# A hybrid S5 and gated-linear-attention step in float32: the loads that bring the gates back move from ScalarE's queue to SyncE's, and two GLA branch tiles take turns with the low parts of S5's output

## What is computed

```python
h = rmsnorm(x, g_mix)
z = h @ w_in        # [u_s5 | q | k | v | r | a_lowrank | gate_s5 | gate_gla]
y5 = s5_mixer(u, ...)                       # diagonal complex state
z5 = gelu(y5);  o5 = z5 * sigmoid(z5 @ w_s5_glu)
og = rmsnorm_per_head(gla_mixer(q, k, v, ...)) * silu(r)
merged = sigmoid(gate_s5) * (o5 @ w_s5_br) + sigmoid(gate_gla) * (og @ w_gla_br)
x = x + merged @ w_out
x = x + square(relu(rmsnorm(x, g_ffn) @ w_ff1)) @ w_ff2
y = rmsnorm(x, g_final)                     # plus the new S5 and GLA states
```

## Time and profile before

| | us |
|---|---|
| median of 3 timed executions | 3113.45 |
| lowest, highest | 3100.98, 3114.78 |
| the profiled execution, its own time | 3107.87 |
| its span, first to last instruction | 3106.1 |
| PE busy (share) | 2974.8 (96%) |
| DVE busy | 1346.8 (43%) |
| POOL busy | 1166.3 (38%) |
| ACT busy | 508.3 (16%) |

### The profile page before, as it was taken

How to read it: one execution, slowest core, us unless ns; L and a number is a source line. 1 busy time by engine, 2 the same in 40 slices (tenths; PEclk the granted TensorE clock), 3 DMA queues, 4 the chain that set the end, 5 groups by cost and what they waited for, 6 DMA issues and landing times.

```text
span 3106.1 us, 47026 instructions
## 1 busy us (share of the span) xinstructions
PE 2974.8 (96%) x19152; PEld 2884.8 (93%) x19152; DVE 1346.8 (43%) x2545; ACT 508.3 (16%) x812; POOL 1166.3 (38%) x917
## 2 busy tenths in 40 slices
PE   5999999889999999999999999998899999999997
PEld 5999988789999999999999999888899999999997
DVE  6645546544353233333463254563534333323334
ACT  3222221231210000000232222213111000000001
POOL 3433322244454443444443332223444443444341
PEclk9999989899999999999999999999999999999998
DMA  3232324422111111111213232444211111111112
GB/s 127 93 113 76 67 86 131 161 99 88 41 51 45 48 45 48 45 48 45 100 52 118 56 78 47 130 131 169 89 52 45 48 46 47 45 48 45 48 45 74
DMA packets 116627, 230.87 MB, mean 74 GB/s; under 512 B 11953, under 2 KB 37329, under 8 KB 115281
## 3 DMA queue, kind: packets, MB, share of 16 engines
q1 hardware_dynamic: 65664, 119.57, 13.3%
q10 hardware_dynamic: 50768, 108.41, 11.0%
HBM read 183.84 MB, written 44.09 MB: 73 GB/s over the span
## 4 chain that ended last, share of the span: by engine, by line
PE 92%; DVE 3%; ACT 2%; ACTq 1%; issue 1%; DMA 0%; DVEq 0%
PE ps L448 28%; PE ps L449 27%; PE ps L450 27%; PE ps L590 2%; PE ps L646 1%; PE ps L667 1%; PE ps L668 1%; PE ps L645 1%; DVE f_h L1339 1%; PE ps L656 1%; PE ps L669 0%; DVE r_o L1339 0%; DVE f_o L1339 0%; PE ps L496 0%; ACTq L1179 0%
## 5 line engine op out<-in xcount | busy, mean ns | idle before, releaser
L430 POOL TENSOR_TENSOR w_hi<-w_raw,zero 128x512 fp32r<-128x512 f32 x456 | 529.3, 1161 | 1829.7 <-PE ps L450 1817.7
L448 PE MATMUL ps<-r_h,w_hi 128*128 128x344 f32 (+1 forms) x2736 | 893.0, 326 | 30.9 <-DVE f_o L1339 15.1
L450 PE MATMUL ps<-r_h,w_lo 128*128 128x344 f32 (+1 forms) x2736 | 882.1, 322 | 0.0
L449 PE MATMUL ps<-r_o,w_hi 128*128 128x352 f32 (+1 forms) x2280 | 735.8, 323 | 0.0
L432 POOL TENSOR_TENSOR w_lo<-w_raw,w_hi 128x512 fp32r<-128x512 f32 x456 | 639.6, 1403 | 64.8
L448 PE MATMUL ps<-r_z,w_hi 128*128 128x344 f32 (+1 forms) x1776 | 583.9, 329 | 25.2 <-DVE f_h L1339 18.5
L449 PE MATMUL ps<-r_h,w_hi 128*128 128x344 f32 (+1 forms) x1800 | 583.0, 324 | 0.0
L450 PE MATMUL ps<-r_z,w_lo 128*128 128x344 f32 (+1 forms) x1776 | 575.2, 324 | 0.0
L448 PEld LDWEIGHTS ps<-r_h,w_hi 128*128 128x128 f32 x2736 | 519.4, 190 | 41.2 <-issue 17.6
L450 PEld LDWEIGHTS ps<-r_h,w_lo 128*128 128x128 f32 x2736 | 519.1, 190 | 0.0
L449 PE MATMUL ps<-r_m,w_hi 128*128 128x344 f32 (+1 forms) x1392 | 449.1, 323 | 0.0
(11 more groups left out here) (337 smaller groups left out, 2727.6 us busy)
## 6 DMA issues: line engine op xcount, KB each, us to landing
w_raw<-wpack SPq DMA_DIRECT2D x456, 256.0 KB, 2.7
f_z<-s_constants ACTq DMA_DIRECT2D x16, 514.0 KB, 3.8
f_h<-s_constants ACTq DMA_DIRECT2D x16, 514.0 KB, 3.8
f_h<-xT ACTq DMA_DIRECT2D x4, 1040.0 KB, 9.0
gate_s_scratch<-f_o ACTq DMA_DIRECT2D x8, 520.0 KB, 3.3
gate_gla_scratch<-f_o ACTq DMA_DIRECT2D x8, 520.0 KB, 3.4
f_h<-gate_gla_scratch ACTq DMA_DIRECT2D x8, 520.0 KB, 8.0
f_h<-gate_s_scratch ACTq DMA_DIRECT2D x8, 520.0 KB, 15.0
```

Source lines behind the costliest of these rows:

```text
L430: pool.tensor_tensor(w_hi[:, s, :], raw, zero[:, :].to_broadcast([P, WB]), ALU.subtract)
L448: pe.matmul(out, wh, h, start=first, stop=False)
L449: pe.matmul(out, wh, l, start=False, stop=False)
L450: return pe.matmul(out, wl, h, start=False, stop=last)
```

## The change

SP takes over the 16 loads of the gates. It issues them once per half, in front of the weight block with the index `JOB_FIRST[JOB["bg", 0]] + RING`, that is the first block behind those of bg 0 to 3, the block of glu 0. Ahead of them it waits for gg 7's last matmul and for all gate stores. ACT no longer waits for these nor issues the loads; its `y_load(3)` and its wait for the y stores stay. On DVE, `gla_branch` is split into one function per block. Where o5_low(0), o5_low(1), gla_branch(4), o5_low(2), o5_low(3), gla_branch(5) stood, the order is now block 0 of bg 4, o5_low(0), block 1, o5_low(1), block 2, o5_low(2), block 0 of bg 5, o5_low(3), blocks 1 and 2; the waits for gg 4 and gg 5 come first.

```diff
--- before.py
+++ after.py
@@ -404,8 +404,21 @@
 
         @block.sync
         def _(sp):
+
+            def gates_back(half):
+                sp.wait_ge(*job_used(half, ("gg", KT_D - 1)))
+                for s in range(2):
+                    sp.wait_ge(gg_stored[s], (half + 1) * 4 * 16)
+                    sp.wait_ge(gs_stored[s], (half + 1) * 4 * 16)
+                for m in range(KT_D):
+                    sp.dma_start(ft(X_LO[half], m), gg_dram[m]).then_inc(gg_landed[m], 16)
+                for m in range(KT_D):
+                    sp.dma_start(ft(X_HI[half], m), gs_dram[m]).then_inc(gs_landed[m], 16)
+
             for half in range(HALVES):
                 for i in range(IT_FF * RING):
+                    if i == JOB_FIRST[JOB["bg", 0]] + RING:
+                        gates_back(half)
                     g = half * HALF_BLOCKS + i
                     if g >= RAW:
                         sp.wait_ge(w_split[(g - RAW) % RING], (g - RAW) // RING + 1)
@@ -1163,26 +1176,13 @@
                         if t == OG_HIGH[h]:
                             act.wait_ge(ocols_read, (half + 1) * PARTS)
                             act.activation(rt(QKV[half] + Q_V, h), r_tile(half, h), ACT.Copy).then_inc(hi_ready, 1)
-                act.wait_ge(*job_used(half, ("gg", KT_D - 1)))
-                gates_back(half, range(1))
                 act.wait_ge(s5dec_ready, half + 1)
                 act.dma_start(s5_dec_out[half], s5_new[:, :, :, :]).then_inc(s5dec_stored, 16)
-
-
-            def gates_back(half, gla, s5=()):
-                for s in range(2):
-                    act.wait_ge(gg_stored[s], (half + 1) * 4 * 16)
-                    act.wait_ge(gs_stored[s], (half + 1) * 4 * 16)
-                for m in gla:
-                    act.dma_start(ft(X_LO[half], m), gg_dram[m]).then_inc(gg_landed[m], 16)
-                for m in s5:
-                    act.dma_start(ft(X_HI[half], m), gs_dram[m]).then_inc(gs_landed[m], 16)
 
             def branches(half):
                 for m in range(KT_S):
                     if m == 1:
                         y_load(half, KT_S - 1)
-                        gates_back(half, range(1, KT_D), range(KT_D))
                     act.wait_ge(yperm_landed[m], (half + 1) * 16)
                     z = ft(WORK[half], m)
                     yp = fv(SIDE[half] + S_Y + m * J * YC, J * YC).rearrange("p (j c) -> p j c", j=J)
@@ -1784,14 +1784,16 @@
                 tt(nim, nim, t1, ALU.add).then_inc(s5dec_ready, 1)
 
             def branches(half):
+                def gla_block(m, b):
+                    (c0, cn), gate, job = BLK[b], ft(X_LO[half], m), ("bg", m)
+                    block_done(half, job, b)
+                    tt(gate[:, c0:c0 + cn], gate[:, c0:c0 + cn], ps[:, block_bank(job, b), 0:cn], ALU.mult
+                       ).then_inc(block_read(half, job, b)[0], 1)
+
                 def gla_branch(m):
                     dve.wait_ge(gg_landed[m], (half + 1) * 16)
-                    gate = ft(X_LO[half], m)
-                    for b, (c0, cn) in enumerate(BLK):
-                        job = ("bg", m)
-                        block_done(half, job, b)
-                        tt(gate[:, c0:c0 + cn], gate[:, c0:c0 + cn], ps[:, block_bank(job, b), 0:cn], ALU.mult
-                           ).then_inc(block_read(half, job, b)[0], 1)
+                    for b in range(len(BLK)):
+                        gla_block(m, b)
 
                 def s5_branch(m):
                     dve.wait_ge(gs_ready, half * KT_D + m + 1)
@@ -1825,12 +1827,12 @@
                     dve.wait_ge(*block_read(half, ("glu", m), 1))
                     dve.wait_ge(*block_read(half, ("glu", m), 2))
                     tt(ft(WORK[half], m), ft(WORK[half], m), ft(A_G, m % 2), ALU.mult).then_inc(full_ready, 1)
-                o5_low(0)
-                o5_low(1)
-                gla_branch(4)
-                o5_low(2)
-                o5_low(3)
-                gla_branch(5)
+                dve.wait_ge(gg_landed[4], (half + 1) * 16)
+                dve.wait_ge(gg_landed[5], (half + 1) * 16)
+                for x in range(2 * len(BLK)):
+                    gla_block(4 + x // len(BLK), x % len(BLK))
+                    if x < KT_S:
+                        o5_low(x)
                 s5_branch(0)
                 gla_branch(6)
                 s5_branch(1)
```

## The result

| | before | after |
|---|---|---|
| median of 6 timed executions, us | 3111.56 | 3090.53 |
| lowest to highest | 3100.98 to 3114.78 | 3084.82 to 3096.72 |
| profiled execution | 3107.87 | 3084.82 |

The ratio is 0.9938 with an interval of 0.9922 to 0.9953. Timed once more beside other kernels it was 0.9953 (0.9939 to 0.9966), so by the ratio the two timings give 19 and 15 us less (the two medians of the table lie 21 us apart): the forecast was 15.

What follows compares the result with a forecast made beforehand. TensorE's matrix work was 92% of the chain, so only its pauses and clock counted. Terms 6.0 + 3.9 - 3.0 + 4.8 + 3.3 = 15.0 us took 3107.9 to 3092.9 us, range 3079 to 3107.

Steps and rivals of the forecast that it cites:

- Third pause and turns: TensorE between glu 3 and bs 0: blocks between low parts remove the 2.39 us pause; bs 0 gains 4.8 and 3.3 us.
- glu 0: Start of glu 0 on TensorE, set by its weights behind the gates: 6.0 us earlier in half 0, 3.9 in half 1.
- the landing of F + 4: First weight block behind bg 0 to 3, needed by glu 0, queued behind 16 gates: lands at 628.0 us, bounds 625 to 631.
- The forecast of the drain from the old queue's rate: SP's queue ahead of glu 0's weights: 9.73 MB at the old trace's near 415 GB/s takes 23.4 us.
- short rows of the stores: Allowance in the queue's drain time for the y stores' short rows: 0.2 us added to 23.4 us.
- Clock: TensorE's slower clock after standing 2 to 3 us before glu 0: 1.5 us lost per half, 3.0 in all.
- First pause: TensorE's wait for gate tile gg 0, now issued by SP: restarts 2.6 us earlier in half 0, 2121.4 against 2123.19 in half 1.
- Second pause: TensorE's 3.89 us wait for bank 0 of bg 2, behind ScalarE's gelus and z_low(2): goes, or leaves up to 1 us.
- Weights in time: Rival: glu 0's weights land by 625.5, no pause or clock loss there; 23.3 us gained, 3084.6 us; chance 0.22.
- rival 1: Glu 0's weights land by 625.5, so no wait or clock loss there; 23.3 us gained, 3084.6 us; chance 0.22.
- Starving stores: Rival: y stores land only after the gates, holding back ScalarE's y_load(3) and gelus; 10.7 us slower, 3118.6 us; chance 0.06.
- Rival 3: Gates load no earlier, glu 0 gains 0 to 2 us per half; only the interleaving's 8.1 us remain, 3100 us; chance 0.14.

Runs made afterwards that it cites:

- the repeat: The same changed kernel timed and profiled again beside other kernels: 0.9953 to the kernel before, stage (gg 7 store to first high part of merged gates, both halves) 155.1 us.
- weights-first run: Changed kernel with the gate loads two weight blocks later in SyncE's program, behind the weights of glu 0 and glu 1: 0.9928 to the kernel before.
- gate 0 early: Changed kernel with weights of glu 0 and 1 ahead of the gates, and gate tile 0 loaded without waiting for gg 7's store: 0.9965 to before.
- all three edits: Changed kernel with gate tile 0 early, weights of glu 0 and 1 first, gates 2 to 15 behind the y stores' landing: 0.9923, again 0.9911.
- gates-only kernel: Changed kernel with VectorE's old order, so only the gate loads moved to SyncE: 0.9986 to the kernel before.

## Why the prediction was right, and where its steps were off

**The sign, the places and the sum held.** 15.0 us were forecast; the stage shows 17.4 and 17.2, the timings 19 and 15. The sum as measured in the stage is 5.3 + 4.0 - 1.6 + 5.6 + 4.1 = 17.4 where the forecast had 6.0 + 3.9 - 3.0 + 4.8 + 3.3. Its errors of up to 1.4 us a term are below the spread of a timing, so that the repeat gave just 15 us is luck. Step by step:

- *Third pause and turns*: 4.8 and 3.3 us forecast, 5.6 and 4.1 measured (alone and in the whole change). VectorE's four low parts took 1.91, 1.23, 1.65 and 1.90 us, 6.7 in all and not the 7.56 of the earlier trace rows, so TensorE never waited for it. The old kernel also had a fourth pause, of 1.22 us (1.19 in half 1), between the third and bs 0; the prediction did not name it, but its sum held it, as it went by the start of bs 0.
- *glu 0*: 6.0 and 3.9 us forecast, 5.3 and 4.0 measured. The term behind it, the landing of F + 4, was forecast 30.8 us behind the gg 7 store (628.0 - 597.16) and measured at 31.7. That it is this landing that ends the last wait is shown by the weights-first run, in which the pauses went and the stage lost 4.8 us. The forecast of the drain from the old queue's rate was the step on which all rested, and it was within a microsecond of the landing, in part because two errors cancelled. The first gate went out 2.81 us behind the store and not 3.49; from there to the landing of F + 4 it took 28.9 us and not 27.35. The term that was too small is the 0.2 us for the short rows of the stores: from 595 to 598.75, with the stores under way, the transfers ran at 305 to 318 GB/s (slices of 1.25 us), and from 600 on at 398 to 426.
- *Clock*: 1.5 us lost per half forecast; 0 and 1.6 measured (from glu 0's first matmul to the last read of glu 3 it took 23.1 us in half 0 and 24.6 in half 1, before 23.0). The price was right where it fell due. In half 0 it didn't: the pause there was 0.80 us and not the 2 to 3 forecast, because the second pause had already taken its part.
- *First pause*: 2.6 and 1.8 us forecast, 2.1 and 1.1 measured (2.2 and 2.0 in the repeat), within the bounds given. In half 0 VectorE began on gate 0 6.03 us behind its issue, not 4.8. The y stores were under way beside it, as they were before; no run tells why it took 1.2 us more.
- *Second pause*: this step failed. It was said to go or to leave up to 1 us; it left 2.32 us in half 0 and 2.79 in the repeat. The stores of y were to land 0 to 4 us later, as the weight loads had in the earlier trace rows; they took up to 6.7 us longer (11.1 against 4.4), so y_load(3) went out 17.09 us behind the store and not at 9.9 to 14.8, and ScalarE stood 5.58 us before the gelu of tile 1, where the prediction had set at most 5 as a sign of being right. One late transfer is not the measure of eight that each meet a gate. It cost nothing only because glu 0 had to wait for its weights anyway: in half 0 TensorE stood 0.80 us there, where 2 to 3 had been expected.

The Trainium skill ("DMA: Bandwidth & Descriptors", section "Queues, rings and completion order") says that each DMA engine goes round the queues packet by packet. From that the prediction had an estimate of some 6 us for the stores; the trace agrees in size, with 6.7. The Trainium skill says in the same section that each DMA engine takes the descriptors of one queue in order. F + 4, which took 15.9 us from issue to landing behind 16 gates, fits that.

**The rivals.** Weights in time (3084.6) did not happen in the change, and the weights-first run shows what it was worth: 4.8 us of the 8.3 that rival 1 put on top. Starving stores: the mechanism came, with y_load(3) at 17.1 us, still short of the 24 us (621 - 597.16) from which it was to decide; gate 0 early showed it at 19.3 us, with a pause of 9.13. Rival 3 (3100) is excluded by the glu 0 starts.

**The profiled difference** of 23.1 us is 6.2 us before the changed code, 17.4 in the two stages, less 0.5 that the rest took longer. Whoever reads the two spans alone puts a quarter of it down to the change wrongly.

## What to carry to other kernels

When a batch of loads moves to another queue, look first at what was short and urgent in the new queue and now stands behind it, and work out its landing from the rate at which the old queue drained: here that gave 31 us against 31.7, and putting two urgent 256 KB blocks ahead of the batch was worth 4.8 us, half of the 9.0 of the move alone. A batch that no longer queues behind small stores runs beside them and delays them, so the wait behind those stores has to be priced too. Curing one of several waits in a row is worth only the distance to the next: gate 0 early made the kernel slower than with the weights first alone (0.9965 against 0.9928), and on top of the other two edits it made the stage 2 to 4 us shorter.

## What the runs showed of the hardware that was not expected

- Eight stores of 66 KB with 528-byte rows, issued while 520 KB loads went out on the other queue, took up to 11.1 us (13.9 with gate 0 early) against 4.4 before.
- A pause of 2.39 us was followed by the lower clock in one half of the kernel before and by none in the other; after the change 2.32 us cost nothing and 2.41 us was followed, 1.5 us into the work, by 3.4 us at 0.53. With all three edits a pause of 2.31 us was followed by 0.69 in the mean of the next 3.0 us. Nor does the first matmul tell it: behind a pause of 3.82 us in half 1 of the repeat it ran at full speed, and 0.8 us later came 3.4 us at the lower level (0.50 from 2108 to 2110); behind one of 3.48 us in the gates-only kernel the slow stretch began at once.
- The unchanged first 590 us differ by up to 8.6 us between executions, with other stretches at the lower clock (from 230 to 270 us it was 1.00 in the change and 0.87 in the weights-first run); comparisons of a few us need marks on both sides of the change.
